# Moving a recurrent pass's gate products into the next pass's first weight slot, and a weight rounding ahead of the gates' sigmoids

## The reference

```
xn = rms_norm(x, norm_pre_w)
z = xn @ w_in                      # u_lru, g_lru, q, k, v, g_attn, ...
u = centred_depthwise_conv(u_lru, conv_w, conv_b)
# rg_lru, once forward and once in reverse, in 16 blocks of 128 features:
gate_r = sigmoid(u_block @ w_r + b_r)
gate_i = sigmoid(u_block @ w_i + b_i)
a = exp(-8 * gate_r * softplus(-lam))
b = sqrt(1 - a*a) * (gate_i * u)
h[t] = a[t] * h[t-1] + b[t]
y_a = (h_forward + h_reverse) * silu(g_lru)
```

## Time and profile before

| | |
|---|---|
| runs of the kernel | 1992.32 us median of 3 (1991.84 to 1992.9) |
| the profiled execution's own time | 1995.17 us |
| its span in the trace | 1993.4 us |
| granted TensorE clock, mean | 0.996 of full speed |
| busy: TensorE matmul, VectorE, ScalarE, GpSimd | 97%, 63%, 55%, 4% |

### The profile page before, as it was taken

The page is one execution under the profiler, slowest core; times in us unless marked ns, Lnnn a source line. Parts: engine busy times, 40 slices in busy tenths (PEclk is TensorE's granted clock), DMA queues, the critical chain, the costliest instruction groups (busy, mean ns, idle before and its releaser), DMA issues.

```text
span 1993.4 us, 32637 instructions
## 1 busy us (share of the span) xinstructions
PE 1935.8 (97%) x13840; PEld 1726.6 (87%) x13840; DVE 1265.2 (63%) x1771; ACT 1104.7 (55%) x1506; POOL 70.1 (4%) x66
## 2 busy tenths in 40 slices
PE   6999999999999999999899999999999999999998
PEld 6999989999888888888798988888889998988887
DVE  5878755555444434654587987555557899775453
ACT  6777745554433333334556578826455656883451
POOL 0111100000000000000000011100000001010000
PEclk9999999999999999999999999999999999999999
DMA  6444454444455555464544343312555444342154
GB/s 226 183 183 183 166 205 160 161 152 143 175 175 205 190 187 190 178 250 169 208 172 149 146 166 112 141 70 104 212 194 208 168 157 140 128 148 86 64 191 148
DMA packets 52272, 328.61 MB, mean 165 GB/s; under 512 B 7968, under 2 KB 10144, under 8 KB 14368
## 3 DMA queue, kind: packets, MB, share of 16 engines
q1 hardware_dynamic: 52128, 326.54, 45.5%
HBM read 320.23 MB, written 6.29 MB: 164 GB/s over the span
## 4 chain that ended last, share of the span: by engine, by line
PE 26%; DVE 11%; ACT 8%; DMA 5%; issue 2%; SPq 0%; DVEq 0%; ACTq 0%
PE z L306 13%; DMA w_raw<-in_w_dram 5%; DVE w_lo L277 4%; PE z L318 4%; ACT w_hi L270 3%; PE aux L2683 2%; DVE acc L2006 2%; DVE conv L2164 1%; PE z L342 1%; PE aux L2592 1%; PE aux L2688 1%; PE z L2521 1%; DVE S L2120 0%; PE aux L2767 0%; DVE S L2145 0%
## 5 line engine op out<-in xcount | busy, mean ns | idle before, releaser
L277 DVE TENSOR_TENSOR w_lo<-w_raw,w_hi 128x2048 fp32r<-128x2048 f32 x274 | 631.3, 2305 | 445.2 <-ACT w_hi L270 444.6
L270 ACT ACTIVATE w_hi<-w_raw 128x2048 fp32r<-128x2048 f32 x286 | 548.1, 1918 | 506.2 <-PE z L318 246.5
L306 PE MATMUL z<-xn_hi,w_hi 128*128 128x256 f32 x2112 | 621.7, 294 | 2.7 <-DVE xn_lo L234 1.5
L306 PE MATMUL z<-xn_hi,w_lo 128*128 128x256 f32 x2112 | 596.4, 282 | 0.0
L306 PE MATMUL z<-xn_lo,w_hi 128*128 128x256 f32 x2112 | 595.6, 282 | 0.0
L306 PEld LDWEIGHTS z<-xn_hi,w_hi 128*128 128x128 f32 x2112 | 398.8, 189 | 22.3 <-issue 13.4
L306 PEld LDWEIGHTS z<-xn_lo,w_hi 128*128 128x128 f32 x2112 | 399.5, 189 | 5.0 <-issue 4.3
L306 PEld LDWEIGHTS z<-xn_hi,w_lo 128*128 128x128 f32 x2112 | 397.9, 188 | 0.0
L318 PE MATMUL z<-w_hi,xn_hi 128*128 128x512 f32 x568 | 226.9, 399 | 0.0
L318 PE MATMUL z<-w_lo,xn_hi 128*128 128x512 f32 x568 | 225.2, 396 | 0.0
L318 PE MATMUL z<-w_hi,xn_lo 128*128 128x512 f32 x568 | 225.1, 396 | 0.0
(11 more groups left out here) (428 smaller groups left out, 2527.9 us busy)
## 6 DMA issues: line engine op xcount, KB each, us to landing
w_raw<-in_w_dram SPq DMA_DIRECT2D x287, 1024.0 KB, 4.8
gate_w<-in_lru_w_dram SPq DMA_DIRECT2D x8, 512.0 KB, 5.6
x_t<-state_dram SPq DMA_DIRECT2D x2, 2048.0 KB, 8.3
x_first<-in_x_dram SPq DMA_DIRECT2D x4, 512.0 KB, 6.5
x_t<-in_x_dram SPq DMA_DIRECT2D x1, 2048.0 KB, 10.6
state_dram<-x_t SPq DMA_DIRECT2D x2, 1024.0 KB, 5.3
pw<-in_pw_dram SPq DMA_DIRECT2D x2, 1024.0 KB, 6.6
state_dram<-x_t SPq DMA_DIRECT2D x8, 256.0 KB, 2.3
```

What stands on the lines that cost most here:

```text
L270: act.activation(self.k.w_hi[:, n % SLOTS], self.k.w_raw[:, m % RAW], ACT.Copy).then_inc(self.s.rounded, 1)
L277: dve.tensor_tensor(self.k.w_lo[:, n % SLOTS], self.k.w_raw[:, m % RAW], self.k.w_hi[:, n % SLOTS].bitcast(F32), ALU.subtract).then_inc(se ...
L306: ins = pe.matmul(out, w[:, kk], x[:, kk], start=kk == 0 and j == 0, stop=kk == KT - 1 and j == 2)
```

## The change

Two edits. On TensorE the gate products of pass i no longer stand at the pass's end: for passes 0 to 6 they are issued inside the first slot of the next pass, ahead of its step `kk` = 6, that is after 18 of its 48 matmuls; for pass 7 after the first slot of the keys. On ScalarE the rounding of slot 4i+3 moves from behind the gates' eight sigmoids to ahead of them. No instruction is added or removed; no semaphore, buffer or count changes.

```diff
@@ ScalarE, step i
                     if i:
                         gate_inputs(i - 1)
+                    ring.round(act, n + 3)
+                    if i:
                         gates(i - 1)
-                    ring.round(act, n + 3)
                     if i:
                         tanhs(i - 1)
                     ring.round(act, n + 4)
@@ TensorE
+                def last_gates(kk, i):
+                    if kk == 6:
+                        gates(i)
+
                 for i in range(LRU_PASSES):
                     for b in range(2):
                         if i:
                             pe.wait_ge(s.ucopied, 2 * (i - 1) + b + 1)
-                            ring.features(pe, 4 * i + b, tile(b), k.xn_hi, k.xn_lo)
+                            ring.features(pe, 4 * i + b, tile(b), k.xn_hi, k.xn_lo, None if b else lambda kk: last_gates(kk, i - 1))
...
-                    gates(i)
 
                 pe.wait_ge(s.ucopied, 2 * LRU_PASSES)
                 for w in range(4):
                     ring.tokens(pe, SLOT_K + w, w, pair(0), k.xn_hi, k.xn_lo)
+                    if w == 0:
+                        gates(LRU_PASSES - 1)
```

## The result

The prediction was 1991.7 us, in 1990.3 to 1994.6. The changed kernel took 2000.67 us (median of 5 runs, 1999.3 to 2002.24) against 1992.9 (1991.84 to 1995.57) for the kernel before, also of 5: a ratio of 1.003, with an interval of 1.0018 to 1.0041. It is **slower by 0.3%**, outside the range and on the side that had a chance of 0.03.

The account below looks back on a forecast made before the run. TensorE, busy for all 26.5 us of a pass, was taken as the bound. It comes 1.8 us earlier, less 1.2 lost at slot 37 to the loop's 4.1 us delay: 1992.32 - 0.6 = 1991.7 us, range 1990.3 to 1994.6.

Parts of the forecast that it names:

- the loop's delay at slot 37: ScalarE and VectorE loop: -1.2 + 0.9 + 4.4 = 4.1 us late at slot 37, against 4.8 us of slack.
- steps 4 to 8: ScalarE waits for the load ahead of the rounding of slot 4i+3: 0.9 us a step, 4.4 us together.
- step 1: VectorE's small operations no longer stretched by GpSimd's products: loop gains 1.2 us, bounds 0 and 2.1.
- step 2: ScalarE waits for slot 11's load: 0.9 us, or 2.6 if the load takes 6.5 again.
- step 3: No wait on ScalarE, since rotary work stretches step 2 and slot 15's load is long there.
- the restart: TensorE at slot 37: 0.1 us charged for restarting behind the new wait of 1.1 us.
- all slacks before slot 37: All hold; the tightest is slot 14's bank, 2.2 us, less 1.6 from TensorE, plus 0.3 from the loop.
- The load of slot 11: Step 2: taken to land in 4.8 us, though it took 6.5 in the old trace.
- Pass 0: TensorE goes on with slot 4 instead of waiting at the gate products, which removes 1.64 us.
- Slower by over 0.2%: Outcome for the whole kernel, told from no change from a loop delay of 8.7 us on; chance 0.03.
- The third rival: Landings of 5.9 us in steps 4 to 8: delay 11.4, TensorE waits every pass, 1999.0 us; chance 0.03.

Follow-up runs that it names:

- half: Changed kernel with the rounding of slot 4i+3 between the fourth and fifth of the eight sigmoids: 1993.86 us, ratio 0.9993 to the kernel before.
- act_only: Changed kernel without the TensorE edit, so only the early rounding on ScalarE: 1994.82 us, ratio 0.9997 to the kernel before.
- steps_to_7: Changed kernel with ScalarE's old order in step 8 alone, first run: 1994.56 us in a single run.
- pe_only: Changed kernel without the ScalarE edit, so only the moved gate products on TensorE: 1993.65 us, ratio 0.9991 to the kernel before.
- steps_to_5: Changed kernel with ScalarE's early rounding in steps 0 to 5 only, old order from step 6 on: 1991.44 us in a single run.
- best: Changed kernel with pass 7's gate products in their old place and early rounding in step 1 only: 1993.73 us, ratio 0.999 to the kernel before.
- whole_again: The changed kernel run again, unchanged: 1996.8 us, ratio 1.0007 to the kernel before.
- steps_to_7_again: Changed kernel with ScalarE's old order in step 8 alone, second run, timed: 1996.69 us, ratio 0.9997 to the kernel before.
- last_gates_old: Changed kernel with the gate products of pass 7 alone back in their old place: 1996.75 us in a single run.
- filled_12: Changed kernel plus 12 matmuls with unused result on TensorE ahead of slot 37: 1998.82 us, ratio 1.0019 to the kernel before.
- whole_third: The changed kernel timed a third time, unchanged: 1998.96 us, ratio 1.0021 to the kernel before.

## Why the prediction was wrong

**The step that failed** is the sum of the loop's delay at slot 37. It was taken as 4.1 us and came out as 7.67: steps 4 to 8 cost 6.53 instead of 4.4, step 1 cost 0.16 instead of gaining 1.2, step 2 cost 0.82 instead of 0.9, and step 3 0.16 instead of nothing. With the slack of 4.73 slot 37 starts 7.67 - 4.73 = 2.94 late instead of 0.6 early. Behind the wait I had put 0.1 us for the restart and nothing for the clock, and 1.63 came. 2.94 + 1.63 = 4.57 is the whole loss.

**What held.** The mechanism, in its places: ScalarE waits for a landing ahead of slots 11, 19, 23, 27, 31 and 35, the delay adds up, all slacks before slot 37 hold, and TensorE pays in one new wait there. The load of slot 11 landed in 4.8 us, as taken. The kind of loss is the one forecast; its size is not. The rule of the Trainium skill that stood against the order (DMA: Bandwidth & Descriptors, its rules for kernel authors: wait late) was borne out: with four sigmoids of cover the loop nearly kept its pace (25.45 against 25.3), with none it lost 1.06 us a step and more.

**Steps 4 to 8, 4.4 us: came out as 6.5.** This is the largest miss, and the term was mis-sized twice (five steps of 0.9 would also be 4.5, not 4.4). I charged each step with the DMA wait alone, 0.9 us. The trace after shows waits of 0.78, 0.78, 0.92 and 0.92 in steps 4 to 7, but the steps grew by 1.06, 1.06, 1.19 and 1.19 (y of passes 3 to 6 starts at 158.57, 183.86, 209.15 and 234.43 in the kernel before), some 0.27 more. ScalarE's rows in step 4 show where. After has these:

```profile
136.37 0.66 ACT L561 ACTIVATE gsig<-z 128x256 f32<-128x256 f32 x2
137.81 1.92 ACT L270 ACTIVATE w_hi<-w_raw 128x2048 fp32r<-128x2048 f32 x1 [0.78 <-DMA w_raw<-in_w_dram]
...
142.12 0.52 ACT L571 ACTIVATE gate_i<-aux,params 128x256 f32<-128x256 f32 x1
142.67 1.71 ACT L581 ACTIVATE tau<-gate_r,scale_t 128x256 f32<-128x256 f32 x4
```

Before, the first sigmoid started 0.55 behind the pair `gsig`, while the pair's last was still running (135.78 - 135.23); the rounding now starts 1.44 behind it, 0.89 more and not 0.78. And the tanhs start 0.55 behind the last sigmoid, where operations of this size otherwise start 0.36 apart. They wait for all eight sigmoids (`taken`) and so for the end of the last one, and no rounding stands between any more. Together that is 0.3; the second part, 0.19, is about what `half` still pays. The last of the steps, step 8, grew by 2.03: its load, issued at 238.7, took 5.7 us and not 4.9, and the wait was 1.75:

```profile
L260 SPq DMA_DIRECT2D w_raw<-in_w_dram x1: 328/328/328, 238.7 to 238.7; - x1
DMA to landing us min/median/max: 5.7/5.7/5.7
```

That wait was 1.75 to 2.42 us in all six traces with the early rounding in step 8 and the TensorE edit, and 0.75 in `act_only`, whose load of slot 35 took 4.7 us. In `steps_to_7` and its repeat that load took 6.1 and 6.4 us without the early rounding in step 8, while `pe_only`, `half`, `steps_to_5` and `best` have 4.8 to 5.0. So the long landing comes with the TensorE edit together with a loop that is late up to step 7, and a landing taken from the old trace is no price for it. Why the load takes longer there is open.

**Step 1, a gain of 1.2 us: came out as a loss of 0.16.** Half of the cause is on ScalarE, which I had not followed there. The old kernel's ScalarE in step 1:

```profile
51.31 0.48 ACT L569 ACTIVATE gate_r<-aux,params 128x256 f32<-128x256 f32 x1
...
54.16 1.99 ACT L270 ACTIVATE w_hi<-w_raw 128x2048 fp32r<-128x2048 f32 x1
59.33 1.71 ACT L581 ACTIVATE tau<-gate_r,scale_t 128x256 f32<-128x256 f32 x4 [3.18 <-DVE scale_t L906]
```

and the same in the kernel after:

```profile
53.95 1.92 ACT L270 ACTIVATE w_hi<-w_raw 128x2048 fp32r<-128x2048 f32 x1 [2.02 <-DMA w_raw<-in_w_dram]
55.77 0.46 ACT L569 ACTIVATE gate_r<-aux,params 128x256 f32<-128x256 f32 x1
...
58.81 1.71 ACT L581 ACTIVATE tau<-gate_r,scale_t 128x256 f32<-128x256 f32 x4
```

VectorE's chain was indeed no longer stretched, and the output gate's product came 1.6 us earlier (57.83 against 59.43). But ScalarE waited 2.02 us for slot 7's landing, a wait that I had left out of this step. The sigmoids came 4.5 later and not some 3, and the tanhs only 0.52 earlier. That was lost in the collision, which moved:

```profile
58.86 4.32 POOL L512 TENSOR_TENSOR gate_i<-gate_i,u_all 128x512 f32<-128x512 f32 x2 [57.81 <-ACT gate_i L571]
```

```profile
58.49 2.28 DVE L277 TENSOR_TENSOR w_lo<-w_raw,w_hi 128x2048 fp32r<-128x2048 f32 x1
62.35 2.98 DVE L277 TENSOR_TENSOR w_lo<-w_raw,w_hi 128x2048 fp32r<-128x2048 f32 x1 [1.58 <-ACT w_hi L270]
```

GpSimd's two products took 4.32 us instead of 2.54 under the first residual, and the second residual 2.98 instead of 2.28 under them: it ends at 65.33, and at 65.17 in the kernel before, which is the 0.16. The section on two separate sides of the Trainium skill's page SBUF — State Buffer calls the port pair of the two engines an exclusive lock that the loser waits out. From it I had taken that the collision would be moved and not removed; the trace agrees, with 0.70 us on the residual against the whole product of 1.27 at most.

**Pass 0, 1.64 us for TensorE: came out as 1.** Slots 2 and 3 waited 0.7 longer in this execution. And slot 4 landed later, so that ScalarE rounded it at 38.84 instead of 37.07; VectorE's convolution stands behind that slot's residual and was as much later, and the moved products still waited 0.5. In `whole_again` they did not wait at all. Here a term was taken as certain that differs by half a microsecond from one execution to the next. It is no part of the miss: once TensorE waits at slot 37, its residual alone sets when that slot starts, and what TensorE had gained before is used up in the wait.

**What a wait does to the clock was not in the sum.** The 1.63 us on slot 37 is more than the whole forecast difference. I had charged "0.1 for the restart". That part held: behind a wait and at full clock slot 37 takes 6.54 us (`steps_to_7_again`, `last_gates_old`, `filled_12`) against 6.41, that is 0.13. The other 1.50 is the clock.

**The chances.** Slower by over 0.2% had 0.03, from a delay of 8.7 us on. With 1.6 us for the clock the point lies at 7.1. The delay was 7.67, with two of its terms (steps 1 and 8) at or beyond the bounds I gave, and the large errors all had one sign, since each was a wait that something used to hide. The range allowed for one or two of them at a time. The third rival was right on the direction, but not by its own road: the loop stayed, barely, under TensorE's 26.5 us a pass up to step 7, and TensorE waited once.

**What stays open.** The profiled executions of before and after account for 4 of the 7.8 us between the medians, and the three measurements of the same change give 0.7 to 3.0 parts in a thousand. The size of the wait at slot 37 (3.4, 2.7, 3.7) and the clock behind it differ among them. The mean clock over all timed executions goes the same way: 0.9916 on average in the first, with the largest cost, 0.9929 in `whole_third` and 0.9935 in `whole_again`. The slow stretch at slot 37 accounts for only 0.24 x 7.10 / 1997.6 = 0.0009 of such a mean, so the rest of the difference lies elsewhere in the kernel; I have no trace of an execution at 2002 us to say where.

## What to carry to other kernels

When an operation that waits for a transfer is moved ahead of work that covered the landing, look for the wait in every step, the first included, and charge it against the loop that issues the next transfer: it returns in each turn and adds up until it is longer than the slack of the engine that sets the end. Then price not only the wait at the end of the chain but what TensorE's clock does behind it. Partial cover (four sigmoids, 0.36 us from one start to the next) was enough here to keep the loop from falling behind, so half the move is the first thing to try.

## What the runs showed of the hardware

- **TensorE's clock behind one wait.** Behind waits of 2.7, 3.4 and 3.7 us at slot 37 it ran partly at 1.2 GHz (mean over 262 to 273 us 0.84, 0.84, 0.69 of 2.4 GHz), behind 0.3, 0.8 (after the filler), 1.4 and 2.4 us it stayed at 2.4. But a wait of 2.04 us at the gate products of pass 0, in `act_only`, was also followed by the lower clock, so the length of the wait alone does not decide it.
- **VectorE and GpSimd stretch each other.** Small VectorE operations of 0.18 us take 1.22 and 1.24 us under a GpSimd product, and GpSimd's two products of 2.54 us take 4.32 when a residual runs as they start.
- **The same load can take up to a third longer with only ScalarE and TensorE reordered.** That of slot 35 took 4.9 us in the kernel before and 5.7 in the kernel after. The moment of issue does not decide it: 6.1 issued at 238.2 (`whole_third`), 4.7 issued at 238.1 (`act_only`).
